# Collecting seven experts' gated rows through an indexed table in DRAM in place of spreading them by matrix products

## The reference

```python
def moe_ffn(h, router_w, router_b, w1, w3, w2):
    logits = h.astype(jnp.float32) @ router_w.astype(jnp.float32) + router_b.astype(jnp.float32)
    top_v, top_i = lax.top_k(logits, TOP_K)
    top_w = jax.nn.softmax(top_v, axis=-1)
    combine = jnp.sum(jax.nn.one_hot(top_i, N_EXPERTS, dtype=jnp.float32) * top_w[..., None], axis=-2)
    combine = combine.astype(h.dtype)
    y = jnp.zeros_like(h)
    for e in range(N_EXPERTS):
        y = y + combine[..., e:e + 1] * swiglu(h, w1[e], w3[e], w2[e])
    return y
```

## Time and profile before

| | us |
|---|---|
| median of 3 runs | 1573.01 |
| lowest and highest | 1572.98, 1574.33 |
| the profiled execution | 1574.65 |
| its span, first to last instruction | 1572.9 |
| first product of the first expert, about | 572.7 |
| TensorE busy | 1544.6 (98% of the span) |
| VectorE, ScalarE, GpSimd busy | 1310.8, 972.1, 49.9 |

### The profile page before, as it was taken

How to read it: one execution, slowest core, us unless ns; L and a number is a source line. 1 busy time by engine, 2 the same in 40 slices (tenths; PEclk the granted TensorE clock), 3 DMA queues, 4 the chain that set the end, 5 groups by cost and what they waited for, 6 DMA issues and landing times.

```text
span 1572.9 us, 19303 instructions
## 1 busy us (share of the span) xinstructions
PE 1544.6 (98%) x7851; PEld 1255.5 (80%) x7851; DVE 1310.8 (83%) x1186; ACT 972.1 (62%) x852; POOL 49.9 (3%) x118
## 2 busy tenths in 40 slices
PE   7999999999999989999999999999999999999997
PEld 3886789999888568888888888888888888888885
DVE  5888888888674479989799899889998989999987
ACT  2532434444444357777777777777777787777775
POOL 5300100000000010000000000000000000000000
PEclk9999999999999999999999999999999999999999
DMA  9765888887823169999999999999999999999990
GB/s 349 267 236 193 282 315 324 306 296 268 307 84 131 54 230 363 371 364 350 330 370 345 365 367 360 335 356 354 358 370 371 342 333 370 349 368 372 344 353 30
DMA packets 158182, 481.04 MB, mean 306 GB/s; under 512 B 4234, under 2 KB 8502, under 8 KB 158086
## 3 DMA queue, kind: packets, MB, share of 16 engines
q1 hardware_dynamic: 156160, 475.02, 82.1%
q0 software_dynamic: 1392, 3.58, 0.7%
q10 hardware_dynamic: 534, 1.13, 0.2%
HBM read 478.66 MB, written 1.05 MB: 305 GB/s over the span
## 4 chain that ended last, share of the span: by engine, by line
PE 95%; DVE 2%; DMA 2%; ACT 1%; issue 0%; SPq 0%; DVEq 0%; ACTq 0%
PE bank L1175 20%; PE bank L1176 20%; PE bank L1177 20%; PE bank L868 6%; PE bank L1053 4%; PE bank L1092 3%; PE bank L1094 3%; PE bank L1093 3%; PE bank L865 3%; PE bank L1068 2%; PE bank L1069 2%; DMA ring<-in_w_mod_dram 2%; PE bank L1070 2%; PE bank L1206 2%; PE bank L1146 1%; PE bank L784 1%
## 5 line engine op out<-in xcount | busy, mean ns | idle before, releaser
L1836 DVE TENSOR_TENSOR ring_low<-ring,w_high 128x2048 fp32r<-128x2048 f32 x336 | 768.5, 2293 | 101.3 <-ACT w_high L2267 94.1
L2267 ACT ACTIVATE w_high<-ring 128x2048 fp32r<-128x2048 f32 x336 | 646.2, 1925 | 238.9 <-PE bank L1177 229.7
L1175 PE MATMUL bank<-w_high,x_high 128*128 128x512 f32 x896 | 355.8, 397 | 0.6 <-issue 0.6
L1176 PE MATMUL bank<-ring_low,x_high 128*128 128x512 f32 x896 | 355.5, 397 | 0.0
L1177 PE MATMUL bank<-w_high,x_low 128*128 128x512 f32 x896 | 352.7, 394 | 0.0
L1175 PEld LDWEIGHTS bank<-w_high,x_high 128*128 128x128 f32 x896 | 168.6, 188 | 41.7 <-DVE ring_low L1836 1.7
L1177 PEld LDWEIGHTS bank<-w_high,x_low 128*128 128x128 f32 x896 | 168.2, 188 | 39.1
L1176 PEld LDWEIGHTS bank<-ring_low,x_high 128*128 128x128 f32 x896 | 168.3, 188 | 37.0
L2206 ACT ACTIVATE tmp_r<-ring 128x1024 fp32r<-128x1024 f32 x84 | 89.2, 1064 | 148.0 <-PE bank L1094 86.5
L1175 PE MATMUL bank<-w_high,act_high 128*128 128x512 f32 x448 | 177.5, 396 | 0.3 <-DVE ring_low L1836 0.3
L1176 PE MATMUL bank<-ring_low,act_high 128*128 128x512 f32 x448 | 175.8, 392 | 0.0
(11 more groups left out here) (353 smaller groups left out, 1690.4 us busy)
## 6 DMA issues: line engine op xcount, KB each, us to landing
ring<-in_moe_w_dram SPq DMA_DIRECT2D x168, 2048.0 KB, 7.9
ring<-in_w_mod_dram SPq DMA_DIRECT2D x23, 2048.0 KB, 10.8
ring<-in_ffn_w_dram SPq DMA_DIRECT2D x21, 2048.0 KB, 14.0
ring<-in_w_in_dram SPq DMA_DIRECT2D x7, 2048.0 KB, 18.7
ring<-in_w_out_dram SPq DMA_DIRECT2D x4, 2048.0 KB, 13.4
ring<-in_w_in_dram SPq DMA_DIRECT2D x4, 1024.0 KB, 14.8
ring<-in_w_mod_dram SPq DMA_DIRECT2D x2, 1024.0 KB, 16.0
gate_row<-in_b_mod_dram POOLq DMA_DIRECT2D x4, 512.0 KB, 7.6
```

Source lines behind the costliest of these rows:

```text
L1175: mm(out_, x_h, w_h, start=first, stop=False)
L1176: mm(out_, x_h, w_l, start=False, stop=False)
L1836: tt_(moe_low(u, m // 2)[:, c], moe_slot(u, m // 2)[:, c], w_high[:, m % HIGHS, :].bitcast(F32), ALU.subtract).then_inc(low_made, 1)
L2267: act(w_high[:, m % HIGHS, :], moe_slot(u, m // 2)[:, c], ACT.Copy).then_inc(high_made, 1)
```

## The change

**Added to routing and set-up.** GpSimd makes `token_of`, each partition's number plus 128 times the column, less 1000. VectorE makes `row_of` = token - 1000 + 256 where the expert is the token's second choice. A table `expert_rows` of 640 rows of 1024 float32 is declared in DRAM: rows 0 to 255 for first choices, 256 to 511 for second choices, the rest for slots that hold no token.

**In each of experts 0 to 6.** The eight products with `spread`, its two transposes, its copy, the split into `y_high` and `y_low` and the four `sums` are gone. In their place TensorE does four products (L1316 of the changed kernel) for each pair of experts with a moving side of two columns (`index_sums`, before unit 10 of the pair's first expert), which give each slot its row number; VectorE turns these into integers (`indices`, two small operations at unit 12). VectorE still multiplies by the gate into `act_m` at units 2 and 4 of the next expert (`row_gate`); then GpSimd issues one indirect DMA that writes the 128 rows of `act_m` to their rows of the table. Before VectorE writes `act_m` again (`product(0)`, unit 9) it waits for that DMA to land.

**Once.** When the first gather is done, GpSimd clears `y_low` and writes it to the 512 rows of the table with four DMAs; VectorE waits for these before it writes `act_low` at unit 14 of the first expert. During the last expert GpSimd reads the 256 rows of first choices into the memory of `x_slots` (`picked`), and after the second addition the 256 rows of second choices into the same place. VectorE adds them into `x` with the routing weights at units 17, 20, 25 and 28 (`add_rows`). The last expert still makes `spread` and combines by products.

The parts of the diff that matter:

```diff
                                            pattern=[[-1, n]], channel_multiplier=1))
                     made(eng.tensor_tensor(m[:, 0:P], m[:, 0:P], ident, ALU.subtract))
+            made(eng.iota(token_of[:, :], [[P, 2 * TT + 1]], base=-int(UNUSED), channel_multiplier=1,
+                          allow_small_or_imprecise_dtypes=True))
             assert consts_made == N_CONSTS
 
             eng.dma_start(router[:, :, :], a["router_w"][0].rearrange("(k p) e -> p k e", p=P)).then_inc(s_router, 16)
@@ -762,6 +793,29 @@
                 eng.wait_ge(split_a.sem, split_a.at(f"x{tt}"))
                 done(eng, eng.tensor_tensor(xn_low[:, tt, :], xn[:, tt, :], xn_high[:, tt, :].bitcast(F32),
                                             ALU.subtract).then_inc(split_v.sem, 1), split_v, f"x{tt}")
+
+            eng.wait_ge(gather_t.sem, gather_t.at("g3", 0))
+            eng.memset(y_low.bitcast(F32), 0.0).then_inc(s_clear, 1)
+            eng.wait_ge(s_clear, 1)
+            for n in range(2 * TT):
+                eng.dma_start(expert_rows[n * P:(n + 1) * P, :], y_low.bitcast(F32)).then_inc(s_zero, 16)
+            eng.wait_ge(s_zero, 2 * TT * 16)
+            for r in range(NE - 1):
+                g, u = r // PAIR, r % PAIR
+                eng.wait_ge(index_v.sem, index_v.at("i", g))
+                eng.wait_ge(row_v.sem, row_v.at("y1", r))
+                eng.indirect_dma_start(expert_rows[:, :],
+                                       bass.IndirectOffsetOnAxis(index[:, g % 2, u * PAIR + u:u * PAIR + u + 1], 0),
+                                       act_m[:, :, :].rearrange("p a n -> p (a n)"), None,
+                                       bounds_check=2 * T + P - 1, oob_is_err=False).then_inc(s_rows_out, 16)
+            eng.wait_ge(s_rows_out, 16 * (NE - 1))
+            eng.wait_ge(fill_v.sem, fill_v.at("l11", NE // PAIR - 1))
+            for n in range(2):
+                if n:
+                    eng.wait_ge(pick_v.sem, pick_v.at("a10"))
+                eng.dma_start(picked, expert_rows[n * T:(n + 1) * T, :].rearrange("(t p) d -> p t d", p=P))\
+                   .then_inc(s_rows_in, 16)
+            eng.wait_ge(s_rows_in, 32)
...
+                def index_sums():
+
+                    eng.wait_ge(route_v.sem, route_v.at("row"))
+                    for v in range(PAIR):
+                        e = g * PAIR
+                        for tt in range(TT):
+                            ins = mm(bank[7][:, v * PAIR:(v + 1) * PAIR], dispatch[:, tt, v, :], row_of[:, tt, e:e + PAIR],
+                                     start=tt == 0, stop=tt == TT - 1)
+                    mark(ins.then_inc(index_t.sem, 1), index_t, "i")
+
+                indexed = q == 0 and u == 0
+                spreads = q == 1 or is_last(q, g, u)
 
                 up(0, "w1", 0)
                 if is_first(q, g, u):
                     eng.wait_ge(route_v.sem, route_v.at("most"))
                 up(0, "w3", 2)
-                if not is_first(q, g, u):
+                if q:
                     combine(old)
 
                 eng.wait_ge(moe_a.sem, moe_a.at("s1", r))
-                up(1, "w1", 0, spread_turn)
-                if not is_first(q, g, u):
+                up(1, "w1", 0, index_sums if indexed else spread_turn if spreads else None)
+                if q:
                     eng.wait_ge(sum_v.sem, sum_v.at("a01", old))
                 turn(0)
-                eng.wait_ge(moe_a.sem, moe_a.at("spread", r))
+                if indexed:
+                    eng.wait_ge(index_v.sem, index_v.at("f", pair(q, g)))
+                if spreads:
+                    eng.wait_ge(spread_a.sem, spread_a.at("s", spread_rep(q, g, u)))
                 turn(1)
                 up(1, "w3", 2)
-                if not is_first(q, g, u):
+                if q:
                     eng.wait_ge(sum_v.sem, sum_v.at("a11", old))
+                elif r:
+                    eng.wait_ge(row_v.sem, row_v.at("y1", old))
                 down(0)
                 down(1)
...
                 done_(nc.vector.memset(chosen[:, :, NE:, :], 0.0).then_inc(route_v.sem, 1), "idle")
+                done_(stt(out=row_of[:, :, :], in0=sel2, scalar=float(T), in1=token_of[:, 0:TT].unsqueeze(2).to_broadcast([P, TT, NE]),
+                          op0=ALU.mult, op1=ALU.add).then_inc(route_v.sem, 1), "row")
                 gate(1, 1, (bank[0], bank[1]))
...
+            def row_gate(half, r):
+
+                eng.wait_ge(unit_used, used_at(r + 1, -1))
+                done(eng, tt_(act_m[:, half, :], bank[4 + half][:, :], gate_row[:, half * W:(half + 1) * W],
+                              ALU.mult).then_inc(row_v.sem, 1), row_v, f"y{half}", r)
+
+            def indices(g):
+
+                eng.wait_ge(index_t.sem, index_t.at("i", g))
+                done(eng, ts_(index_f[:, :], bank[7][:, 0:2 * PAIR], token_of[:, 2 * TT:2 * TT + 1], UNUSED, ALU.min, ALU.add).then_inc(index_v.sem, 1),
+                     index_v, "f", g)
+                done(eng, nc.vector.tensor_copy(index[:, g % 2, :], index_f[:, :]).then_inc(index_v.sem, 1), index_v, "i", g)
+
+            def add_rows(n):
+
+                if n % 2 == 0:
+                    eng.wait_ge(s_rows_in, 16 * (n // 2 + 1))
+                tt = n % 2
+                done(eng, stt(out=x[:, tt, :], in0=picked[:, tt, :], scalar=route_c[:, 4 + n // 2, tt, 0:1], in1=x[:, tt, :],
+                              op0=ALU.mult, op1=ALU.add).then_inc(pick_v.sem, 1), pick_v, f"a{tt}{n // 2}")
+
...
                         if not first or m >= HIGHS:
                             low(r, u, m)
                         if m in (2, 4) and not first:
-                            y_gate((m - 2) // 2, old, r)
-                        if m in (3, 5) and not first:
+                            if q:
+                                y_gate((m - 2) // 2, old, r)
+                            else:
+                                row_gate((m - 2) // 2, old)
+                        if m in (3, 5) and q:
                             y_rest((m - 3) // 2, old)
-                        if m == 10 and not first:
+                        if m == 10 and q:
                             sums(old, old_weight, 0)
-                        if m == 11 and not first:
+                        if m == 11 and q:
                             sums(old, old_weight, 1, 2)
-                        if m == 12 and not first:
+                        if m == 12 and q:
                             sums(old, old_weight, 3)
+                        if m == 12 and not q and u == 0:
+                            indices(g)
+                        if m == 9 and not first and not q:
+                            eng.wait_ge(s_rows_out, 16 * r)
+                        if m in (17, 20, 25, 28) and last:
+                            add_rows((17, 20, 25, 28).index(m))
                         if m in (9, 10):
                             product(m - 9)
...
                         if m == 14:
+                            if first:
+                                eng.wait_ge(s_zero, 2 * TT * 16)
                             act_lows(0)
                             act_lows(1)
...
-                        if m in (3, 5) and not first:
+                        if m in (3, 5) and q:
                             y_first((m - 3) // 2, old)
                         if m in (6, 7):
                             gated(m - 6)
-                        if m == 13:
-                            eng.wait_ge(moe_t.sem, moe_t.at("spread", r))
-                            done(eng, act(spread[:, :], bank[7][:, 0:T], ACT.Copy).then_inc(moe_a.sem, 1),
-                                 moe_a, "spread", r)
+                        if m == 13 and (q or last):
+                            at = spread_rep(q, g, u)
+                            eng.wait_ge(spread_t.sem, spread_t.at("s", at))
+                            done(eng, act(spread[:, :], bank[7][:, 0:T], ACT.Copy).then_inc(spread_a.sem, 1),
+                                 spread_a, "s", at)
```

51 lines of the change are left out of this document (39 added, 12 removed).

## The result

| | before | after |
|---|---|---|
| median, us | 1572.99 (1572.7 to 1574.33, 4 runs) | 1552.95 (1550.19 to 1555.29, 4 runs) |
| ratio, 95% interval | | 0.9864 (0.9849 to 0.9879) |
| profiled execution, its span | 1574.65, 1572.9 | 1555.29, 1553.6 |
| first to last product with an expert's weights | 572.7 to 1559.5: 986.8 | 572.1 to 1540.4: 968.3 |

The change is faster by 20.0 us, where 12.0 were forecast and the range allowed 15. Of the 19.3 us between the spans, 18.5 lie between the first and the last of the 4032 products with the experts' weights (last line of the table, from the starts of these products in the trace).

What follows compares the result with a forecast made beforehand. TensorE was taken to bound the kernel; -12.8 + 0.2 + 0.2 + 0.4 = -12.0 us takes the median from 1573.0 to 1561.0. The range was 1558 to 1568, holding about 0.84.

Steps and rivals of the forecast that it cites:

- the paragraph on the bound: In the experts TensorE sets the pace; an instruction leaving its list shortens the kernel by its own time.
- combine, between units 7 and 8: On TensorE, the eight combine products go in seven of eight experts: 7 x 1.83 = 12.8 us less.
- transposes out, index products in: On TensorE: seven pairs of transposes go, 1.6 us less; four groups of index products come, 1.8; net 0.2 us more.
- the waits of the earlier trace: TensorE's weight loads wait for VectorE in three places, 1.3 us in all; their removal was counted at nothing.
- more than forecast: Rival: index products cost nothing and TensorE's waits for VectorE go; 1559 us (1558 to 1559.5), chance 0.05.
- the four additions, last expert: VectorE, behind units 17, 20, 25 and 28: about 1.3 us each, 5.2 in all; 0.4 us more taken.
- row_of, ahead of the experts: In the routing, one more small VectorE operation delays the first expert's first product: 0.2 us more.
- the list in the forecast: Signs of being right, such as no gap between units 7 and 8 and a stream above 365 GB/s.
- The stream: Rival: in the experts 362 GB/s of DMA traffic is the ceiling, so only 6 us gained; 1567 us, chance 0.06.
- The port: Rival: each scatter holds the port VectorE's low needs, 7 us lost; 1568 us, chance 0.13 including a slow first scatter.
- The late scatter: Rival: scatter lands after the 14.2 us allowed before product(0) stalls TensorE, 27 us lost; 1588 us, chance 0.10.
- The second read: Last expert: issued after unit 20's addition, wanted 14 us later behind unit 25; 11 us allowed, so it fits.

Runs made afterwards that it cites:

- the shift alone: Kernel before plus an unused 32-byte tensor at token_of's place, so every later tensor lies 32 bytes further on; 1566.14 us, ratio 0.9954.
- the change at the old places: Changed kernel with token_of inside the 32 bytes of eps_col, so the products' operands lie where they lay before; 1561.63 us, ratio 0.9917.

## Why the prediction was right and wrong

**The step that failed** is a sentence of the paragraph on the bound: "An instruction that leaves TensorE's list in the experts shortens the kernel by its own time, as long as VectorE and the weight stream can go at the new pace." That took for granted that all others on TensorE keep theirs. The sum priced every instruction the diff adds or takes, and none for the 20 bytes of token_of, which changed the distance of 4032 products that the diff doesn't name. What the runs showed in its place: the shift alone gains 8.0 us by the medians, 4.7 in the experts' stretch, with no change of work, and the change at the old places gains 12.5, where 12.0 were forecast. The places are the missing term: 6.2 us of the changed kernel's stretch.

**The terms of the sum**, from the gaps between units, the kernel before with the shift against the changed one (same places):

| term | forecast | measured |
|---|---|---|
| combine, between units 7 and 8 | -12.8 | 7 x 1.83 = -12.8 |
| transposes out, index products in | +0.2 | 4 x 0.22 - 3 x 0.25 = +0.1 |
| the waits of the earlier trace rows | 0 (in the rival "more than forecast") | 3 x 0.42 = -1.3, at units 14 and 15 |
| the four additions, last expert | +0.4 | +0.3, around units 22 and 23 |
| row_of, ahead of the experts | +0.2 | 0.17 busy; not to be read in the start of the experts |

With 0.1 in small pieces the sum in the experts is -13.8; at the old places it is -12.3, beside the forecast's -12.2 (there the waits gave back 0.9, and some units were slower by 0.03 each). The start of the experts can't show 0.2 us: over the sixteen profiles it lies between 569.9 and 575.3, and it moves for other reasons: a step of VectorE's set-up (lru_k) starts at 43.7 us in the kernel before and 46.4 in the changed one, and ahead of the experts the granted clock fell to 0.50 for 3.4 us five times in each of these two, six at the old places, four with the shift alone. For the same reason I compare stretches, not spans: the profile of the change at the old places has a span only 9.9 us shorter, with a start 2.4 later, and it is the slowest of its four runs.

**The transposes and the index products.** A pair of transposes taken out gave back 0.14 us between units 9 and 10 and 0.11 within unit 10, 0.25 against the 0.23 from the earlier trace rows. Four index products took 0.22 more than the pair in whose place they stand, 0.47 a group, where 4 x 0.115 = 0.46 was taken from the transpose's row. Both sizes held.

**What was right of the list in the forecast**: no gap between units 7 and 8; an expert without gathers at 119.7 us, 119.9 forecast (by luck: it is 120.5 at the old places, since that item had left out the index products, and the faster products made up for them); weight loads waiting 1.2 us in all; product(0) waiting for no DMA; the indirect DMA landing at 9.2, between 9 and 11; a stream of 376 GB/s, above 365.

**The rivals.** The stream is not the bound: it gave 376 GB/s over 122 us. The Trainium skill gives some 358 as a core's limit, half of what it gives for the memory that two cores share (page "DMA: Bandwidth & Descriptors", section "Specifications"). Here one core runs, and the trace is above that figure. The ring's blocks land later, 8.5 us in place of 7.9, and nobody waits. The port: one low beside the indirect DMA of 1312.05 and the next, timeline of VectorE in the changed kernel:

```profile
1311.25 2.29 DVE L1910 TENSOR_TENSOR ring_low<-ring,w_high 128x2048 fp32r<-128x2048 f32 x1
1313.81 2.29 DVE L1910 TENSOR_TENSOR ring_low<-ring,w_high 128x2048 fp32r<-128x2048 f32 x1 [0.27 <-ACT w_high L2373]
```

2.29 us both, and none of the experts' took over 2.33. The indirect DMA cost VectorE nothing that the trace shows. The Trainium skill's rule (page "SBUF — State Buffer", section "Who interferes with whom"), which agreed with the earlier trace rows for a subtraction on POOL, does not show for an indirect DMA that reads 128 indices. The late scatter: 10.5 us against a room of 13.5 to 14.0, 3 us to spare, where the forecast had 3.2 to 5.2. The range was drawn around these. The case "more than forecast" was summed wrongly: its own terms, 1.8 us for the index products and 1.3 for the waits, make 1557.9 out of 1561.0, not 1559. Of the two, the waits went (1.3 us at the shifted places) and the index products kept their price. No case had a mechanism by which the time could fall to 1553.

**The additions** took 1.28 us each (1.3 forecast). The second read was issued at 1478.0, when the addition behind unit 20 was done, and used at 1490.2, 12.2 us later. The reads landed in 10.3 us (11 allowed), and nobody waited:

```profile
1476.44 1.28 DVE L1937 SCALAR_TENSOR_TENSOR x<-x_slots,route_c,x 128x1024 f32<-128x1024 f32 x1
...
1490.22 1.28 DVE L1937 SCALAR_TENSOR_TENSOR x<-x_slots,route_c,x 128x1024 f32<-128x1024 f32 x1
```
